# Linear state-space scan: score blocks computed only where they are not zero, and the masked copy of a step put between two halves of the next step's decayed queries and keys

## The reference, cut to what matters

```
S_t = diag(f_t) S_{t-1} + k_t^T v_t,   o_t = q_t S_t,   k_t = 1 - f_t
in a chunk:  b = cumsum(log f)
scores[t, s] = sum_d q[t,d] k[s,d] exp(b[t,d] - b[s,d])   for s <= t, else 0
o[t]         = (q[t] exp(b[t])) S  +  sum_s scores[t, s] v[s]
S            = exp(b[last]) S  +  sum_s (k[s] exp(b[last] - b[s]))^T v[s]
```

## Time and profile before

| | us |
|---|---|
| median of 3 runs | 2024.71 (2020.85 to 2026.29) |
| profiled execution, its own time | 2023.5 |
| its span in the trace | 2021.7 |
| the stage `hgrn` in the trace | 460 to 689 |

### The profile page before, as it was taken

The page is one execution under the profiler, slowest core; times in us unless marked ns, Lnnn a source line. Parts: engine busy times, 40 slices in busy tenths (PEclk is TensorE's granted clock), DMA queues, the critical chain, the costliest instruction groups (busy, mean ns, idle before and its releaser), DMA issues. The chain is left out here.

```text
span 2021.7 us, 32126 instructions
## 1 busy us (share of the span) xinstructions
PE 1940.0 (96%) x11104; PEld 1609.6 (80%) x11104; DVE 1467.0 (73%) x2035; ACT 1225.7 (61%) x1962; POOL 277.2 (14%) x391
## 2 busy tenths in 40 slices
PE   7989999999999899999999999999999999999995
PEld 6878888887888676778888888887888888888882
DVE  5447765648999588877411355468999999999985
ACT  5453467427788488754222333336888888888873
POOL 0220012110000021111000000001222222222210
PEclk9999999999999999999999999999999999999997
DMA  6493334446565460343334523337999999999998
GB/s 207 162 313 109 105 115 146 151 172 180 181 183 178 151 199 27 116 135 134 115 120 138 163 84 110 116 132 272 384 386 382 384 378 382 380 386 383 394 370 323
DMA packets 177237, 441.98 MB, mean 219 GB/s; under 512 B 20768, under 2 KB 100000, under 8 KB 151264
## 3 DMA queue, kind: packets, MB, share of 16 engines
q1 hardware_dynamic: 145168, 341.19, 47.1%
q0 software_dynamic: 31952, 99.25, 13.3%
HBM read 359.64 MB, written 94.37 MB: 225 GB/s over the span
## 5 line engine op out<-in xcount | busy, mean ns | idle before, releaser
L113 PE MATMUL cross_ot_ps<-w_w_high,cross_o_high 128*128 128x512 f32 x528 | 213.4, 404 | 4.6 <-DVE w_w_low L2952 2.8
L115 PE MATMUL cross_ot_ps<-w_w_high,cross_o_low 128*128 128x512 f32 x528 | 207.1, 392 | 0.0
L2952 DVE TENSOR_TENSOR cross_low_up<-cross_raw_up,w_w_high 128x2048 fp32r<-128x2048 f32 x66 | 148.3, 2288 | 9.4 <-ACT w_w_high L2719 9.3
L2952 DVE TENSOR_TENSOR w_w_low<-cross_raw_gate,w_w_high 128x2048 fp32r<-128x2048 f32 x68 | 152.3, 2278 | 0.0
L2952 DVE TENSOR_TENSOR cross_low_down<-cross_raw_down,w_w_low 128x2048 fp32r<-128x2048 f32 x64 | 143.4, 2282 | 0.0
L2719 ACT ACTIVATE w_w_high<-cross_raw_gate 128x2048 fp32r<-128x2048 f32 x68 | 126.2, 1907 | 0.0
L113 PEld LDWEIGHTS cross_ot_ps<-w_w_high,cross_o_high 128*128 128x128 f32 x528 | 99.9, 189 | 29.9 <-DVE w_w_low L2952 7.1
L2719 ACT ACTIVATE w_w_high<-cross_raw_up 128x2048 fp32r<-128x2048 f32 x66 | 122.5, 1907 | 0.3 <-issue 0.3
L2719 ACT ACTIVATE w_w_low<-cross_raw_down 128x2048 fp32r<-128x2048 f32 x64 | 119.0, 1914 | 0.0
L115 PEld LDWEIGHTS cross_ot_ps<-w_w_high,cross_o_low 128*128 128x128 f32 x528 | 99.7, 189 | 21.5
L114 PE MATMUL cross_ot_ps<-w_w_low,cross_o_high 128*128 128x512 f32 x264 | 104.2, 395 | 0.0
(11 more groups left out here) (539 smaller groups left out, 5495.1 us busy)
## 6 DMA issues: line engine op xcount, KB each, us to landing
cross_raw_gate<-in_w_gate_dram SPq DMA_DIRECT2D x66, 1024.0 KB, 7.7
cross_raw_up<-in_w_up_dram SPq DMA_DIRECT2D x66, 1024.0 KB, 9.5
cross_raw_down<-in_w_down_dram SPq DMA_DIRECT2D x64, 1024.0 KB, 9.0
front_pair_raw<-in_w_in_dram SPq DMA_DIRECT2D x9, 1024.0 KB, 7.0
cross_y_kept<-y_rows SPq DMA_DIRECT2D x16, 512.0 KB, 10.4
front_raw<-in_w_in_dram SPq DMA_DIRECT2D x10, 512.0 KB, 5.5
k_t<-front_staged POOLq DMA_DIRECT2D x20, 256.0 KB, 2.7
lf_t<-front_staged_lf POOLq DMA_DIRECT2D x20, 256.0 KB, 3.0
```

Source lines behind the costliest of these rows:

```text
L113: pe.matmul(out, lhs[0], rhs[0], start=first, stop=False)
L115: return pe.matmul(out, lhs[1], rhs[0], start=False, stop=last)
L2952: dve.tensor_tensor(w_low[s][:, cols], raw[s][:, cols], w_high[s][:, cols].bitcast(F32), ALU.subtract).then_inc(w_low_done[s], 1)
```

## The change

`scores(n)` no longer multiplies with halves that are zero. Each level's product is now cut to the block of 64 or 32 key tokens by 64 or 32 query tokens where it is not zero, and is written, not accumulated: for level 64 one 64x64 block for each head, for level 32 two 32x32 blocks, for level 16 four 32x32 diagonal blocks (the zeros inside them are still needed), and for the centred product four 32x32 diagonal blocks in place of one 128x128. What no product writes must be zero, so `levels_ps` is now a tile for each direction, zeroed once, and `centred_ps` one for both, zeroed once, both by DVE as its first two instructions. POOL zeroes only the level 16 planes.

On DVE, `decayed` is cut in two, `decayed_levels` and `decayed_rest`, and `mask(n + 1)` stands between the two for step n + 2; before, it came after both and after the split.

The diff, without the lines that only name semaphores:

```diff
--- before.py
+++ after.py
@@ -1165,21 +1165,19 @@
         whole = m.sb("whole", [P, 2, HEADS])
         minus_mid = m.sb("minus_mid", [P, HEADS])
         raw, w_high, w_low = zip(*early_split)
-        kt_ps, o_ps, st_ps = (m.ps(s, [P, HW]) for s in ("kt_ps", "o_ps", "st_ps"))
-        s_ps = m.ps("s_ps", [P, 2, 2, HEADS // 2, P])
-        by_head = lambda t: t.rearrange("p (a b t) -> p a b t", b=2, t=P)
-        levels_ps, centred_ps = (s_ps[:, :, c].rearrange("p b a t -> p a b t") for c in range(2))
+        kt_ps, o_ps, st_ps, centred_ps = (m.ps(s, [P, HW]) for s in ("kt_ps", "o_ps", "st_ps", "centred_ps"))
+        levels_ps = m.ps("levels_ps", [P, 2, HW])
         acc = m.ps("acc", [P, 2, 512])
         w_in, w_stored = ([m.sem(f"{s}{u}") for u in range(2)] for s in ("w_in", "w_stored"))
         w_high_done, w_low_done, acc_ready, staged_done, later_in = (
             m.sem(s) for s in ("w_high_done", "w_low_done", "acc_ready", "staged_done", "later_in"))
         x_in, v_in = ([[m.sem(f"{s}{u}{d}") for d in range(2)] for u in range(2)] for s in ("x_in", "v_in"))
...
@@ -1240,9 +1238,8 @@
             def _(pool):
                 for t, half in ((q_dec, early), (k_dec, late)):
                     for u in range(2):
-                        for j, w in enumerate(LEVELS):
-                            halves = t[:, u, j].rearrange("p (g two l) -> p g two l", two=2, l=w)
-                            pool.memset(halves[:, :, half[u]], 0.0).then_inc(zeros_done, 1)
+                        halves = t[:, u, n_lev - 1].rearrange("p (g two l) -> p g two l", two=2, l=base)
+                        pool.memset(halves[:, :, half[u]], 0.0).then_inc(zeros_done, 1)
                 for p in range(parts):
                     if p == parts - 1:
                         pool.drain()
@@ -1257,7 +1254,7 @@
 
                 def key_tokens(i, u):
                     act.wait_ge(scores_ready, ready(2 * i + u))
-                    act.activation(by_head(s_t[:]), levels_ps, ACT.Copy).then_inc(level_scores_done, 1)
+                    act.activation(s_t[:], levels_ps[:, u], ACT.Copy).then_inc(level_scores_done, 1)
                     act.activation(k_tok[:], kt_ps[:], ACT.Copy).then_inc(kt_done, 1)
 
                 def decays(i, u):
@@ -1329,6 +1326,8 @@
             @block.vector
             def _(dve):
                 dve.sem_inc(base_done, PRIME)
+                dve.memset(levels_ps[:].rearrange("p u c -> p (u c)"), 0.0).then_inc(levels_zeroed, 1)
+                dve.memset(centred_ps[:], 0.0).then_inc(levels_zeroed, 1)
 
                 def differences(i, u):
                     n = 2 * i + u
@@ -1355,11 +1354,11 @@
                                       bv[:, :, CENTRE:CENTRE + 1].to_broadcast([P, HW // base, base]),
                                       ALU.subtract).then_inc(diff_done, 1)
 
-                def decayed(i, u):
+                def decayed_levels(i, u):
                     n = 2 * i + u
                     q, k = x[i % 2][:, u, 0], x[i % 2][:, u, 1]
                     if n == 0:
-                        dve.wait_ge(zeros_done, 4 * n_lev)
+                        dve.wait_ge(zeros_done, 4)
                     dve.drain()
                     dve.wait_ge(decay_done, n + 1)
 
@@ -1369,6 +1368,10 @@
                         e, qd, kd = (halves(t[:, u, j]) for t in (decay, q_dec, k_dec))
                         dve.tensor_tensor(qd[:, :, late[u]], e[:, :, late[u]], halves(q)[:, :, late[u]], ALU.mult)
                         dve.tensor_tensor(kd[:, :, early[u]], e[:, :, early[u]], halves(k)[:, :, early[u]], ALU.mult)
+
+                def decayed_rest(i, u):
+                    n = 2 * i + u
+                    q, k = x[i % 2][:, u, 0], x[i % 2][:, u, 1]
                     dve.tensor_tensor(q_dec[:, u, n_lev], q, decay[:, u, centred], ALU.mult)
                     dve.tensor_tensor(k_dec[:, u, n_lev], k, uncentre[:, u], ALU.mult)
                     dve.tensor_copy(whole[:, u].unsqueeze(2),
@@ -1382,8 +1385,9 @@
                     n = 2 * i + u
                     dve.wait_ge(scores_ready, ready(n))
                     dve.wait_ge(level_scores_done, n + 1)
-                    dve.copy_predicated(by_head(s_t[:]), where_i[:, u].unsqueeze(1).unsqueeze(1).to_broadcast(
-                        [P, HEADS // 2, 2, P]), centred_ps).then_inc(s_done, 1)
+                    dve.copy_predicated(s_t[:].rearrange("p (h t) -> p h t", h=HEADS),
+                                        where_i[:, u].unsqueeze(1).to_broadcast([P, HEADS, P]),
+                                        centred_ps[:].rearrange("p (h t) -> p h t", h=HEADS)).then_inc(s_done, 1)
 
                 def carry(i, u):
 
@@ -1405,21 +1409,25 @@
 
                 differences(0, 0)
                 differences(0, 1)
-                decayed(0, 0)
+                decayed_levels(0, 0)
+                decayed_rest(0, 0)
                 dve.memset(state[:], 0.0).then_inc(state_done, PRIME)
                 split_low(2)
                 differences(1, 0)
                 mask(0, 0)
-                decayed(0, 1)
+                decayed_levels(0, 1)
+                decayed_rest(0, 1)
                 split_low(3)
                 for n in range(slots):
-                    if n:
-                        mask(n // 2, n % 2)
                     if n + 3 < slots:
                         differences((n + 3) // 2, (n + 3) % 2)
                     carry(n // 2, n % 2)
                     if n + 2 < slots:
-                        decayed(n // 2 + 1, n % 2)
+                        decayed_levels(n // 2 + 1, n % 2)
+                    if n + 1 < slots:
+                        mask((n + 1) // 2, (n + 1) % 2)
+                    if n + 2 < slots:
+                        decayed_rest(n // 2 + 1, n % 2)
                     for p in range(4, parts):
                         if split_in[p] == n:
                             split_low(p)
@@ -1437,23 +1445,29 @@
                         pe.wait_ge(s_done, n)
                         pe.wait_ge(kt_done, n)
                     else:
-                        pe.wait_ge(zeros_done, 4 * n_lev)
+                        pe.wait_ge(zeros_done, 4)
+                        pe.wait_ge(levels_zeroed, 2)
                     for h in range(HEADS):
                         cols = slice(h * P, (h + 1) * P)
                         pe.transpose(kt_ps[:, cols], k_dec[:, u, n_lev + 1, cols], ident[:])
 
+                    def block(into, j, h, s_at, t_at, size):
+                        rows, cols = (slice(h * P + at, h * P + at + size) for at in (s_at, t_at))
+                        return pe.matmul(into[s_at:s_at + size, cols], k_dec[:, u, j, rows], q_dec[:, u, j, cols],
+                                         start=True, stop=True)
+
+                    wide, narrow = LEVELS[0], 2 * base
                     for h in range(HEADS):
-                        cols = slice(h * P, (h + 1) * P)
-                        pe.matmul(s_ps[:, h % 2, 1, h // 2], k_dec[:, u, n_lev, cols], q_dec[:, u, n_lev, cols],
-                                  start=True, stop=True)
-                    for pair in range(HEADS // 2):
-                        for j, w in enumerate(LEVELS):
-                            for h in (2 * pair, 2 * pair + 1):
-                                for at in range(0, P, 2 * w):
-                                    cols = slice(h * P + at, h * P + at + 2 * w)
-                                    done = pe.matmul(s_ps[at:at + 2 * w, h % 2, 0, pair, at:at + 2 * w],
-                                                     k_dec[:, u, j, cols], q_dec[:, u, j, cols],
-                                                     start=(j == 0), stop=(j == n_lev - 1))
+                        block(levels_ps[:, u], 0, h, early[u] * wide, late[u] * wide, wide)
+                    for h in range(HEADS):
+                        for at in range(0, P, 2 * narrow):
+                            block(levels_ps[:, u], 1, h, at + early[u] * narrow, at + late[u] * narrow, narrow)
+                    for h in range(HEADS):
+                        for at in range(0, P, narrow):
+                            block(levels_ps[:, u], n_lev - 1, h, at, at, narrow)
+                    for h in range(HEADS):
+                        for at in range(0, P, narrow):
+                            done = block(centred_ps, centred, h, at, at, narrow)
                     done.then_inc(scores_ready, 1)
 
                 def output(i, u):
```

8 lines of the change are left out of this document (4 added, 4 removed).

## The result

| | median us | runs |
|---|---|---|
| before | 2023.34 | 10 (2020.38 to 2026.29) |
| after | 2030.3 | 10 (2028.36 to 2032.18) |

The ratio is 1.0035, with a 95% interval of 1.0027 to 1.0043. The forecast was 2022.0 with a range of 2015 to 2029; the time lies above the range. The profiled execution of after took 2028.36 us, its span is 2026.6 (before 2023.5 and 2021.7).

What follows compares the result with a forecast made beforehand. DVE was taken to set the pace until about 661 us, PE only in the last three steps. The terms -2.1 + 2.5 + 1.4 - 2.7 - 1.8 gave -2.7 us, from 2024.7 to 2022.0, range 2015 to 2029.

Steps and rivals of the forecast that it cites:

- DVE sets the pace, PE's saving brings nothing in the middle: Stage until about 661 us: DVE nearly full, so PE's 1.76 us saved per step become idle time.
- The scores take 1.6 us: PE, each step: scores in small blocks take 1.6 instead of 3.36 us.
- The clears, +1.4: DVE, stage start: two clears ahead of the first scan, covered by nothing, add 1.4 us.
- The masked copy doesn't wait in its new place: DVE, each turn: reached 3.31 us after the carry began, ACT's copy ready at 2.7 us, so no wait.
- The last three steps, -4.5: Stage end: output of step 17 released earlier, -2.7 us, and faster scores of step 19, -1.8 us.
- The split, +2.5: DVE, middle: carries of steps 5, 8 and 15 wait 0.62, 1.26 and 0.62 us for PE's work behind the split.
- Rival 5, the clock, chance 0.04: PE idles 1.8 us in each step, so its clock falls; at half clock above 2100 us; chance 0.04.
- The waits of the middle, -2.1: DVE, middle: 2.1 us of waits for other engines go, since PE has 1.8 us of room each step.

Runs made afterwards that it cites:

- e1: After, with the split on DVE moved from the turn's end to ahead of the carry; 2016.8 us, ratio 0.9967.
- e3: Before, with the new DVE order alone (masked copy between the two halves) and scores in whole blocks; 2034.76 us, ratio 1.0055.
- e4: After, with 40 unused transposes on PE before the wait for the splits of parts 6, 8 and 13; 2023.93 us, ratio 1.0008.
- e9: After, measured once more with nothing altered; 2032.85 us, ratio 1.0055.
- e7: e1 with scores in whole blocks and no clears; 2018.79 us, ratio 0.9981.
- e11: e10 with scores in whole blocks, without the small blocks; 2019.22 us, ratio 0.9988.
- e10: e1 with the 112 units of the big product in the first 18 steps, none in the last two; 2011.3 us, ratio 0.9952.

## Why the prediction was wrong

- *DVE sets the pace, PE's saving brings nothing in the middle*: right. e1's middle is 166.5 us with 20.7 us of PE idle.
- *The scores take 1.6 us*: right. From the transposes to the big product it is 2.08 us (541.21 to 543.29) where 0.44 + 1.6 were expected and the earlier trace rows have 3.80.
- *The clears, +1.4*: +1.2 until carry 0, and 0.91 and 0.48 us for themselves. Clearing PSUM costs as much as the clearing of the state did. Between the starts of the first clear and the first scan it is 1.36 us; 0.2 of them are gone by carry 0.
- *The masked copy doesn't wait in its new place*: right in after, where it waits once, in the last step. With whole blocks (e3) it does.
- *The last three steps, -4.5*: measured -4.5, and term by term: -2.8 from carry 16 to 18 (forecast -2.7), -1.7 from 18 to 19 (-1.8).
- *The split, +2.5*: **this term failed.** The three carries that it named are the ones that waited, but for 8.5 us. Its own mechanism has the size given (e4: 0.48 and 1.17 us). It took PE's work behind the split at full clock, from a row where PE had waited 0.87 us, though the change lets PE wait far longer, 5.1 to 5.6 us, at this very place. At step 5 that work took 5.06 us, and 3.48 where the clock was held (e4).
- *Rival 5, the clock, chance 0.04*: here the reasoning went wrong. It spread PE's idle time evenly, 1.8 us a step, and compared it with a stretch of 18.32 us busy in 20. The idle time doesn't all stay where it arises: PE's limits are the operands and the masked copy, which are written a turn or more ahead, so that part of the room becomes a lead, until PE meets something that is made late. Counted from carry 0, the transposes of step 5 begin 3.5 us sooner in after than in before (525.38 and 528.01), and the scores of that step are 1.7 shorter; together this is the 5.2 us by which the wait for the split grew (0.45 to 5.61). In before PE met this split with 0.45 us of wait, so nothing showed it. The price of the rival was wrong as well: in the middle the clock fell around three places and cost 6 us, not 80.
- *The waits of the middle, -2.1*: about twice too large. The 2.1 us were what the count of DVE's work left over; only 1.2 of them were waits for another engine. In e1 DVE waits for nobody in the middle, and it takes 166.5 us: 1.1 less than before, and 1.0 more than the 165.5 of the count.

The lines for the lead of step 5: PE in before (the transposes, the first product behind the split), then PE in after (the transposes; its product is the line at 536.15 in the section on the result). Carry 0 is at 487.31 and 488.15.

```profile
528.01 0.60 PE L1443 MATMUL hgrn_kt_ps<-kept_ident,hgrn_k_dec 128*128 128x128 f32 x4
...
535.27 0.50 PE L113 MATMUL hgrn_acc<-mem_high,mem_next_high 128*128 128x512 f32 x1 [0.45 <-DVE mem_next_low L1403]
```

```profile
525.38 0.66 PE L1452 MATMUL hgrn_kt_ps<-kept_ident,hgrn_k_dec 128*128 128x128 f32 x4 [0.40 <-DVE hgrn_q_dec L1382]
```

In time: -2.7 us were forecast and +7.0 measured between the medians. Of the 9.7 us between, the stage of the profiled execution explains 7.1 (4.4 and not -2.7). The medians of the two measurements of after lie 7 and 10.7 us above before, while the profiled executions show a stage longer by 4.4 and 4.0; both were the fastest of their runs. What the other executions add, 2.6 and 6.7 us, is not settled; no trace of one exists. Their mean granted clock is on record: 0.979 to 0.981 for after, with no order by time, and in e9 0.980 for the fastest and 0.978 for the two slowest (2034.97 and 2035.26), which may point the same way.

## What to carry to other kernels

Time that is taken from an engine which doesn't set the pace need not be spread over its work: here two thirds of it (16.4 of 25.1 us) piled up in front of the next thing that another engine made late. Look for that place, and read there what the work behind it costs at the low clock; then move that producer forward, or fill the room with work from where the engine is the bound. With the producer moved forward alone the small blocks brought 3.3 us of stage (e7 to e1), with the room filled as well 8.7 (e11 to e10). All edits together are 10.9 us faster than before (e10), where the change by itself is 7 us slower.
